# Reordering three engines around one block boundary of a hybrid decoder block: u's evacuation, q's low weights, the clearing of a bank

## The reference

```
xn   = rms_norm(h, norm1)
q, k, v, z, b, a, c, u, b', gate_a, gate_b = split(xn @ w_in)
q, k, v = silu(causal_conv(q, k, v)); q, k l2-normalised per head (8 heads of 128)
o    = chunk_gated_delta_rule(q, k, v, decay(a), sigmoid(b))     # chunks of 64 tokens
y_a  = (rms_norm(o) * silu(z)) @ w_dn_out
y_b  = (b' * causal_conv(c * u)) @ w_sc_out
h    = h + (sigmoid(gate_a) * y_a + sigmoid(gate_b) * y_b) @ w_o
out  = rms_norm(h + (silu(gate) * up) @ w_down, final_norm)[16:]  # gate, up from rms_norm(h) @ w_gate_up
```

## Time and profile before

| | |
|---|---|
| median of 3 runs | 1093.54 us (1093.45 to 1094.25) |
| the profiled execution | 1093.89 us, of which the span is 1091.9 |
| TensorE busy | 1068.8 us (98%) |
| VectorE, ScalarE, GpSimd busy | 344.0, 457.1, 549.6 us |
| granted TensorE clock, mean over the span | 0.997 |
| chain that ended last | PE 91%, DVE 3%, issue 2%, POOL 2% |
| TensorE matmuls, POOL's `w_lo` | 8275; 322 operations of 1309 ns mean |

### The profile page before, as it was taken

The page is one execution under the profiler, slowest core; times in us unless marked ns, Lnnn a source line. Parts: engine busy times, 40 slices in busy tenths (PEclk is TensorE's granted clock), DMA queues, the critical chain, the costliest instruction groups (busy, mean ns, idle before and its releaser), DMA issues.

```text
span 1091.9 us, 20341 instructions
## 1 busy us (share of the span) xinstructions
PE 1068.8 (98%) x8275; PEld 911.6 (83%) x8275; DVE 344.0 (32%) x642; ACT 457.1 (42%) x1062; POOL 549.6 (50%) x481
## 2 busy tenths in 40 slices
PE   7999999999999999999999999999999999999997
PEld 6989898989989898978888888878888888888886
DVE  6344554545464646361100112221111121200001
ACT  5655555564646464642422233442233333232232
POOL 4353444535353536363544555655565555554553
PEclk9999999999999999999999999999999999999999
DMA  4221222222212122112342322222222322233222
GB/s 181 69 89 60 80 67 69 79 69 61 87 60 88 60 69 80 59 62 76 101 169 79 106 86 97 97 97 95 87 90 96 97 97 97 97 97 97 91 83 77
DMA packets 28811, 95.43 MB, mean 87 GB/s; under 512 B 2984, under 2 KB 5288, under 8 KB 28720
## 3 DMA queue, kind: packets, MB, share of 16 engines
q1 hardware_dynamic: 27520, 91.77, 25.7%
q10 hardware_dynamic: 1200, 2.38, 0.7%
HBM read 92.03 MB, written 2.11 MB: 86 GB/s over the span
## 4 chain that ended last, share of the span: by engine, by line
PE 91%; DVE 3%; issue 2%; POOL 2%; ACT 0%; DMA 0%; DVEq 0%; POOLq 0%
PE bank L974 90%; POOL w_lo L314 1%; DVE tm L764 1%; DVE am L698 1%; DVE qkv L703 0%; DVE qkv L711 0%; POOL malev L301 0%; DVE cv L711 0%; DMA h_in<-h_t 0%; DVE tm L698 0%; PE bank L1153 0%; PE bank L1147 0%; DVE ma L773 0%; DVE x_lo L715 0%; POOL mt L342 0%
## 5 line engine op out<-in xcount | busy, mean ns | idle before, releaser
L314 POOL TENSOR_TENSOR w_lo<-w_raw,w_hi 128x512 fp32r<-128x512 f32 x322 | 415.8, 1309 | 472.4 <-ACT w_hi L403 472.3
L974 PE MATMUL bank<-x_hi,w_hi 128*128 128x258 f32 (+2 forms) x896 | 249.1, 336 | 12.8 <-POOL w_lo L314 7.6
L974 PE MATMUL bank<-x_lo,w_hi 128*128 128x258 f32 (+2 forms) x896 | 231.1, 316 | 0.0
L974 PE MATMUL bank<-x_hi,w_lo 128*128 128x258 f32 (+2 forms) x896 | 231.1, 316 | 0.0
L403 ACT ACTIVATE w_hi<-w_raw 128x512 fp32r<-128x512 f32 x322 | 187.3, 620 | 97.9 <-PE bank L974 97.5
L974 PEld LDWEIGHTS bank<-x_hi,w_hi 128*128 128x128 f32 x896 | 146.5, 190 | 27.4 <-DVE raw L698 7.1
L974 PE MATMUL bank<-og_hi,w_hi 128*128 128x512 f32 x416 | 164.9, 396 | 0.0
L974 PE MATMUL bank<-og_hi,w_lo 128*128 128x512 f32 x416 | 164.5, 395 | 0.0
L974 PE MATMUL bank<-og_lo,w_hi 128*128 128x512 f32 x416 | 164.5, 395 | 0.0
L974 PEld LDWEIGHTS bank<-x_hi,w_lo 128*128 128x128 f32 x896 | 147.7, 189 | 11.1
L974 PEld LDWEIGHTS bank<-x_lo,w_hi 128*128 128x128 f32 x896 | 148.3, 190 | 8.9
(11 more groups left out here) (259 smaller groups left out, 1283.7 us busy)
## 6 DMA issues: line engine op xcount, KB each, us to landing
w_raw<-w_stream SPq DMA_DIRECT2D x162, 512.0 KB, 3.3
h_in<-h_t SPq DMA_DIRECT2D x4, 528.0 KB, 4.9
h<-h_t ACTq DMA_DIRECT2D x1, 2048.0 KB, 10.1
h_in<-gc_dram SPq DMA_DIRECT2D x7, 264.0 KB, 3.1
out<-h SPq DMA_DIRECT2D x4, 256.0 KB, 2.9
out<-h SPq DMA_DIRECT2D x2, 384.0 KB, 2.6
cst<-consts SPq DMA_DIRECT2D x1, 512.0 KB, 8.1
h_in<-gc_dram ACTq DMA_DIRECT2D x1, 264.0 KB, 3.2
```

Source lines behind the costliest of these rows:

```text
L314: nc.gpsimd.tensor_tensor(low_weights(n)[:, at], w_raw[:, n % 3, at], high_weights(n)[:, at].bitcast(f32), ALU.subtract).then_inc(wlo_read ...
L974: return nc.tensor.matmul(o, w, x, start=start, stop=stop)
```

## The change

Three places are reordered. On GpSimd, in each block b, both halves of the low weights for the next block (q of the next head, or gb after the last) stand behind the level 0 mask of step 0 and ahead of steps 1 and 2, where before one half stood behind each. On VectorE the meta tokens' operations move from step 0 to step 1, so that the readings of u stand ahead of them. On ScalarE the clearing of `dbank[2]` moves from step 2 to step 3, behind the copy of level 0's product.

```diff
@@ GpSimd, the loop over blocks
             for n in range(STREAM + 1):
+                weights_first = n < MAIN and BLOCKS[n][0] == "b"
                 for q in range(4):
+                    if q == 1 and weights_first:
+                        split_weights(n + 1, 0)
+                        split_weights(n + 1, 1)
                     if n >= DELTA_FROM:
                         next(delta, None)
-                    if q in (1, 2) and n + 1 < STREAM:
+                    if q in (1, 2) and n + 1 < STREAM and not weights_first:
                         split_weights(n + 1, q - 1)
@@ ScalarE, delta_steps
-                        if step == 2:
-                            act.wait_ge(mkv_ready, h + 1)
-                            nc.scalar.activation(dbank[2][:, 0:256].rearrange("p (a c) -> p a c", c=128),
-                                                 ones.unsqueeze(1).broadcast_to([128, 2, 128]), ACT.Copy,
-                                                 scale=0.0).then_inc(cleared, 1)
                         if step == 4:
                             act.wait_ge(mt_turned, h + 1)
...
                             ins.then_inc(pb_ready, 1)
+                        if step == 3:
+                            act.wait_ge(mkv_ready, h + 1)
+                            nc.scalar.activation(dbank[2][:, 0:256].rearrange("p (a c) -> p a c", c=128),
+                                                 ones.unsqueeze(1).broadcast_to([128, 2, 128]), ACT.Copy,
+                                                 scale=0.0).then_inc(cleared, 1)
@@ VectorE, delta_steps
                             dve.wait_ge(t_ready, h + 1)
                             nc.vector.transpose(flat(um), flat(tm)).then_inc(u_ready, 1)
+                        if step == 1:
                             dve.wait_ge(mpre_done, h + 1)
                             dve.wait_ge(mx_ready, h + 1)
                             dve.wait_ge(km_root, h + 1)
```

## The result

The changed kernel takes 1100.53 us (median of 4 runs, 1099.92 to 1103.73) against 1093.89 for the kernel before (median of 4 runs, 1093.45 to 1094.30). The ratio is 1.0067, 95% interval 1.0047 to 1.0087: slower by 6.6 us, where 1093.9 was forecast and 1096.0 was the end of the range. The profiled execution took 1100.68 us, its span is 1098.2 us against 1091.9. In the code of the changed kernel the lines behind the edits are four to five numbers on: L974 is L979, L885 is L890, L889 is L894, L764 is L768.

The account below looks back on a forecast made before the run. TensorE was taken to bound the kernel, with 6.8 us of waits to gain. Seven heads at -0.11 us and head 0 at +0.41 summed to a 0.36 us loss, 1093.9 us; range 1086.3 to 1096.0.

Parts of the forecast that it names:

- What bounds: TensorE, busy 98% of the span; in the eight heads it waits only for `w_lo`, 6.6 us in all.
- the two late arrivals at the block's start: POOL's `w_lo` (131.22) and VectorE's last reading of u (130.83) arrive just before TensorE's block start at 131.33.
- the next thing late: At step 4 TensorE needs POOL's five small operations; its `mt` load comes at 133.09 instead of 132.98.
- (2): After the held `mult`, today's distances put the first `mt` at 131.03, tap 0 at 131.40, first `malev` at 131.50.
- (3): Tap 0, with 0.10 lead, wins against the first `malev` and ends at 132.11; `malev` 1 can run from 131.97.
- the sum for one head: Chain from held `mult` to TensorE's `mt` load: 0.11 us lost per head, 0.41 gained in head 0.
- The rows of the lock: Profile rows read as VectorE operations with two SBUF inputs and POOL operations excluding each other, to about 0.02 us.
- Rivals 1: First `malev` wins against tap 0: 3.4 us gained in all, 1090.1 us; chance 0.24.
- Rival 3: Tap 1 takes the ports ahead of the second `malev`: 1.8 us lost, 1095.3 us; chance 0.22.
- rival 2: POOL's small operations are not held: the full 6.8 us gained, 1086.7 us; chance 0.14.
- Part 3: ScalarE's clearing of the bank, 0.39 us, moved behind the level 0 copy: taken as 0, at most 3.1 us.
- "Can only lose by adding" waits: On TensorE, busy 98% at high granted clock, a change gains only by removing waiting time, loses only by adding some.

Follow-up runs that it names:

- e1: The changed kernel with a wait on `mkv_ready`, open when VectorE reaches it, ahead of tap 0 of u's convolution; 1092.08 us, ratio to before 0.9986.
- e6: The changed kernel with a wait on `u_ready`, settled long before, ahead of tap 0; 1100.94 us, ratio to before 1.0065.
- e8: The changed kernel with tap 0's addend from PSUM in heads 1 to 7 (does not compute the reference); 1090.42 us, ratio to before 0.9972.
- e7: The kernel before with only the clearing of the bank moved to step 3; 1093.79 us, ratio to before 0.9999.
- e3b: The kernel before with the moves on VectorE and ScalarE alone, low weights left in place; 1130.41 us, ratio to before 1.0334.
- e2: The changed kernel with a wait on `mt_ready` ahead of tap 0, keeping both taps off POOL's five small operations; 1090.95 us, ratio to before 0.9976.

## Why the prediction was wrong, point by point

- What bounds, and the two late arrivals at the block's start: right. The block starts 0.37 us behind level 0, u and both halves of `w_lo` are in time.
- u's readings free of POOL (1.52 forecast, 128.80 to 130.30 measured), half 0 held by L764 (1.49), half 1 from 129.79 where 129.42 + 0.37 was to be (the head starts 0.37 later): right.
- `mult` held by `w_lo` half 1 for 0.5 us or so, and the next thing late being `mt`, at step 4: right in kind; the pair took 0.83, where 0.6 to 0.7 had been forecast. With it the chain starts 0.1 late.
- The step that failed is (2) with (3) of the sum for one head: "the first `mt` starts at 131.03, tap 0 at 131.40, the first `malev` at 131.50", and tap 0 would meet `malev` alone. The starts were right to 0.1 (131.50 and 131.86 less 0.37 are 131.13 and 131.49), but not that the earlier start wins: the first `mt` stands in the sum at its free 0.21 us, without a term for being held. The first `mt`, 0.36 us ahead of tap 0 in the record, was held to tap 0's end, and so the second to tap 1's and all three `malev` behind both. The load of `mt` came at 3.53 behind level 0, where 133.09 - 130.16 = 2.93 was forecast: 0.60 per head, eight times, 4.8 of the 6.6 us that the forecast missed. A further 0.8 is the 0.1 us per head whose cause is open; I have no place for the last 1.0, but for 0.35 by which the two medians of the kernel before differ. e1, e6 and e8 show that it was tap 0, that an open wait in front of it undoes it, and that its second SBUF input is what does it.
- I had worked out the lead from recorded starts, and took every row in which two operations competed. In each of the rows I used, VectorE's operation had an open wait, so none could show the early grip. What I needed was a two-input operation without one, behind a predecessor that leaves the ports alone, and a POOL operation starting meanwhile; I had no such row, and the range had to allow for it. The rule I cited says on this point more than I used: the Trainium skill ("SBUF — State Buffer", Who interferes with whom) has it that issue order decides who blocks. The trace agrees if "issued" means something earlier than the recorded start. How much earlier it does not say: when `mt` started at 131.50, the record has `mkdec` running (131.35 to 131.68), and `mvb`, tap 0's direct predecessor, only starts at 131.61. So either tap 0 had the ports from two places back, or `mt` reads 0.11 us or more behind its recorded start, when `mvb` was already running. No run separates the two.
- The rows of the lock fit "to about 0.02 us" in all cases but one: by the hand-over used for the others (0.14 before the end of VectorE's operation) the level 0 mask beside `tm` should take 0.97 us and takes 1.09, before and after the change alike. The forecast does not hang on it.
- Rivals 1 and 3 differed from the forecast in the order of `malev` and the taps, rival 2 had nothing held; none had the first `mt` held. Rival 3 had the right sign and was too small: 1.8 us lost against 6.6.
- Part 3, the clearing at nothing: right (e7).
- "Can only lose by adding" waits was not all: in e3b the wait of 3.8 us cost another 1.7 by the granted clock behind it. In the changed kernel, with 1.5 us of wait, this did not happen.

## What to carry to other kernels

When an operation is moved on one of VectorE and GpSimd, list for both which neighbours have two SBUF inputs, and what stands directly behind a short operation without an open wait: that one may already hold the ports. Short operations on which TensorE waits are best kept beside readings of PSUM, or protected by making the long neighbour wait for their semaphore, as in e2; a wait that is settled protects nothing. And before a stall is removed, the next deadline is to be recomputed for everything that the edit pushed back, at the pace of held operations and not of free ones.

## What the runs showed of the hardware

- A POOL operation that takes 0.21 us free took 1.18 when a VectorE operation with two SBUF inputs was recorded 0.36 or 0.37 us later (changed kernel, e3b and e6, all eight heads), and not with one of its inputs in PSUM (e8: 0.21) or an open wait ahead of it (e1: 0.21).
- How far ahead of its recorded start the early grip reaches is open. It was seen only with two SBUF inputs and without an open wait, and always behind a predecessor with one SBUF input at most. Behind a predecessor that holds the ports itself it did not happen: in the kernel before, L711 at 16.66 us stands unwaited behind such an operation, and POOL's `x_lo`, started at 16.20, went first (L711 took 1.82 us).
- Two VectorE operations of 16x1 elements are held like wide ones: 0.83 us for the pair instead of 0.17 beside `w_lo`.
- A wait of TensorE of 3.8 us was followed by 3.5 us at a granted clock of 0.52 (e3b); one of 1.5 us was not (changed kernel).
- Not explained: in e1 tap 1 stood waiting from 132.00 and did not come between the last `malev` and the level 1 mask.
